# The first wide block of weights of a transformer kernel: its high part split between the roots and the tokens' high parts, its low part made by VectorE in four steps

## The reference

```python
h = jnp.concatenate([meta, x], axis=1)          # 16 + 512 tokens, 1024 wide
xn = rmsnorm(h, ln1_w[l])
proj = xn @ w_in[l]
dq, dk, dv, gq, gk, gv, gr, zf, zb = jnp.split(proj, splits, axis=-1)
log_g_f = jax.nn.log_sigmoid((zf @ gla_gate_w2_f[l] + gla_gate_b_f[l]).astype(f32)) / GLA_TAU
go = gla_bidirectional(gq * GLA_DK ** -0.5, gk, gv, log_g_f, log_g_b)
```

## Time and profile before

| | us |
|---|---|
| median of three executions | 2353.7 |
| lowest, highest | 2352.68, 2358.15 |
| the profiled execution | 2351.1 |
| span of its instructions | 2349.8 |
| PE busy in it | 2178.6 (93%) |
| DVE, ACT, POOL busy | 1522.6, 896.7, 739.2 |

### The profile page before, as it was taken

The page is one execution under the profiler, slowest core; times in us unless marked ns, Lnnn a source line. Parts: engine busy times, 40 slices in busy tenths (PEclk is TensorE's granted clock), DMA queues, the critical chain, the costliest instruction groups (busy, mean ns, idle before and its releaser), DMA issues.

```text
span 2349.8 us, 31219 instructions
## 1 busy us (share of the span) xinstructions
PE 2178.6 (93%) x12667; PEld 1270.3 (54%) x12743; DVE 1522.6 (65%) x2554; ACT 896.7 (38%) x1066; POOL 739.2 (31%) x548
## 2 busy tenths in 40 slices
PE   5999889888999988999999999999979988999998
PEld 3565554455565555777656555555545455444444
DVE  2557663338979999999578888888868174433002
ACT  4433452333333423666433333333333354444110
POOL 4311001311414342322123333334417401544540
PEclk8999899998999999999999999999979999999999
DMA  5114562215868777778899999999721311232300
GB/s 195 66 46 144 179 213 74 91 37 197 319 245 290 269 275 256 290 289 310 301 361 375 376 383 379 379 384 371 271 101 61 106 55 36 72 108 108 143 36 36
DMA packets 194479, 483.39 MB, mean 206 GB/s; under 512 B 10672, under 2 KB 93648, under 8 KB 188320
## 3 DMA queue, kind: packets, MB, share of 16 engines
q1 hardware_dynamic: 154624, 334.65, 40.1%
q0 software_dynamic: 39712, 146.74, 16.5%
HBM read 428.92 MB, written 52.43 MB: 205 GB/s over the span
## 4 chain that ended last, share of the span: by engine, by line
PE 54%; DVE 24%; DMA 14%; ACT 3%; issue 3%; POOL 2%; SPq 1%; DVEq 0%; ACTq 0%; POOLq 0%
PE psum L559 14%; PE psum L560 14%; PE psum L558 14%; DMA expert_act<-act_dram 11%; DVE weight_low L1968 6%; DMA rows_b<-peer_v_dram,row_index 2%; DVE row_sum L2197 2%; PE psum L956 2%; POOL weight_low L2518 2%; PE psum L748 1%; DVE hidden_low L2364 1%; DVE rows_a L2184 1%; DVE rows_b L2184 1%; DVE expert_act L2359 1%; PE psum L839 1%
## 5 line engine op out<-in xcount | busy, mean ns | idle before, releaser
L558 PE MATMUL psum<-x_high,weight_high 128*128 128x384 bf16 (+3 forms) x1826 | 640.7, 351 | 39.9 <-DVE weight_low L1968 24.1
L559 PE MATMUL psum<-x_low,weight_high 128*128 128x384 bf16 (+3 forms) x1845 | 647.3, 351 | 12.1 <-DVE x_low L1859 5.9
L560 PE MATMUL psum<-x_high,weight_low 128*128 128x384 bf16 (+3 forms) x1844 | 645.5, 350 | 0.6
L1270 ACT ACTIVATE weight_high<-weight_stage 128x4096 bf16<-128x4096 f32 (+2 forms) x100 | 356.2, 3562 | 241.7 <-PE psum L560 129.1
L2518 POOL TENSOR_TENSOR weight_low<-weight_stage,weight_high 128x512 bf16<-128x512 f32 (+1 forms) x237 | 308.8, 1337 | 431.3 <-ACT weight_high L1270 431.3
L558 PE MATMUL psum<-hidden_high,weight_high 128*128 128x384 bf16 x1024 | 335.4, 328 | 10.0 <-DVE hidden_low L2364 10.0
L559 PE MATMUL psum<-hidden_low,weight_high 128*128 128x384 bf16 x1024 | 335.4, 328 | 0.0
L560 PE MATMUL psum<-hidden_high,weight_low 128*128 128x384 bf16 x1024 | 335.3, 327 | 0.0
L1968 DVE TENSOR_TENSOR weight_low<-weight_stage,weight_high 128x4096 bf16<-128x4096 f32 x69 | 304.8, 4417 | 36.2 <-ACT weight_high L1270 36.2
L558 PEld LDWEIGHTS psum<-x_high,weight_high 128*128 128x128 bf16 (+1 forms) x1856 | 186.2, 100 | 210.8 <-DVE weight_low L1968 28.6
L560 PEld LDWEIGHTS psum<-x_high,weight_low 128*128 128x128 bf16 (+1 forms) x1856 | 185.9, 100 | 158.9 <-issue 13.4
(11 more groups left out here) (349 smaller groups left out, 2969.9 us busy)
## 6 DMA issues: line engine op xcount, KB each, us to landing
weight_stage<-peer_u_dram SPq DMA_DIRECT2D x32, 2048.0 KB, 8.6
weight_stage<-peer_v_dram SPq DMA_DIRECT2D x32, 2048.0 KB, 11.6
weight_stage<-mlp_w_dram SPq DMA_DIRECT2D x16, 2048.0 KB, 8.0
weight_stage<-ada_w_dram SPq DMA_DIRECT2D x12, 2048.0 KB, 8.0
act_dram<-norm_value SPq DMA_DIRECT2D x128, 192.0 KB, 10.1
gate_dram<-gate_matrices SPq DMA_DIRECT2D x12, 2048.0 KB, 12.2
gates<-gate_dram SPq DMA_DIRECT2D x32, 768.0 KB, 16.7
expert_act<-act_dram SPq DMA_DIRECT2D x32, 768.0 KB, 18.5
```

What stands on the lines that cost most here:

```text
L558: self.nc.tensor.matmul(out, left[0], right[0], start=first, stop=False)
L559: self.nc.tensor.matmul(out, left[0], right[1], start=False, stop=False)
L560: return self.nc.tensor.matmul(out, left[1], right[0], start=False, stop=last)
L1270: nc.scalar.activation(k.block_view(m.w_high, n % SPLITS, n), k.block_view(m.w_stage, n % STAGES, n), ACT.Copy).then_inc(*s.w_high.up(n))
```

## The change

ACT now splits block 1 between the roots and the tokens' high parts. The low part of block 1 is DVE's: four subtractions of 128x8x128, one for each column group, the first ahead of DVE's share of z, the other three behind it. PE waits for one group at a time: a new counter `first_low` for groups 0 to 2, `w_low[1]` for the last. The functions of the diff besides `first_low` are `by_vector`, PE's and ACT's `column_tiles`, ACT's `norm` and DVE's `projections`.

```diff
+        self.first_low = self.new("first_block_split")
     def by_vector(self, n):
-        return (self.block["da_q"] <= n <= self.block["da_v"] or ...
+        return (n == self.block["gla_qk"] or self.block["da_q"] <= n <= self.block["da_v"] or ...
...
         m_rows = 2 * GLA_RANK if name == "z" else P
-        if f == 0:
+        if name == "gla_qk":
+            n = self.k.block[name]
+            self.nc.tensor.wait_ge(*(s.first_low.at(f) if f < 3 else s.w_low[1].at(n)))
+            self.block = (n,) + tuple(self.k.block_view(part, n % SPLITS, n) for part in (m.w_high, m.w_low))
+        elif f == 0:
             self.block = self.weights(name)
...
         if parts_free is not None:
             nc.scalar.wait_ge(*parts_free)
+        if j == "ln1":
+            self.split(k.block["gla_qk"])
         for t in range(KT):
             nc.scalar.wait_ge(*s.normed.at(j, t))
...
-        if f == 0:
+        if f == 0 and name != "z":
             self.begin(name)
...
-        self.column_tiles("z", 0)
+        for f in range(4):
+            self.first_low(f)
+            if f == 0:
+                self.column_tiles("z", 0)
...
+    def first_low(self, f):
+        nc, s, k, m = self.nc, self.s, self.k, self.m
+        n, at = k.block["gla_qk"], slice(P * f, P * (f + 1))
+        low, whole, high = (k.block_view(buffer, slot, n)[:, :, at] for buffer, slot in (
+            (m.w_low, n % SPLITS), (m.w_stage, n % STAGES), (m.w_high, n % SPLITS)))
+        nc.vector.wait_ge(*s.w_high.at(n))
+        nc.vector.tensor_tensor(low, whole, high, ALU.subtract).then_inc(
+            *(s.first_low.up(f) if f < 3 else s.w_low[1].up(n)))
```

More of the change, by code:

```diff
@@ L462, in by_vector @@
     def by_vector(self, n):
-        return (self.block["da_q"] <= n <= self.block["da_v"] or self.block["w_out", 0] <= n <= self.block["w_out", 1]
+        return (n == self.block["gla_qk"] or self.block["da_q"] <= n <= self.block["da_v"] or self.block["w_out", 0] <= n <= self.block["w_out", 1]
                 or self.block["u", 0] <= n <= self.block["v", NG - 1])
```

## The result

| us | before | after |
|---|---|---|
| median of six executions each | 2353.19 | 2339.73 |
| lowest, highest | 2348.94, 2358.15 | 2332.01, 2340.83 |
| the profiled execution | 2351.1 | 2340.46 |
| its span | 2349.8 | 2339.2 |

The ratio of the times is 0.9934, 95% interval 0.992 to 0.9949, so 12 to 19 us are gained. Two more measurements of the same kernel gave 0.9947 (0.9928 to 0.9965) and 0.9939 (0.9926 to 0.9952). The forecast was 2341, with 2336 to 2347.

A forecast was written before the change was run, and what follows sets the result against it. PE was taken as the bound (54% of the chain), pausing 10.4 us for POOL's weight_low; 9.8 (earlier start) + 1.5 (group 0's clock) + 1.0 (gates' clock) = 12.3 us off the 2353.7 median gives 2341, range 2336 to 2347.

The forecast's parts named there:

- The split at no cost: ACT's moved split runs from 18.9 to 22.5 us, costed at nothing, with some 0.2 us of cover for a late load.
- Rival A: Block 1's load lands late, at 24.1; first token tile 5.6 us late, gain 6.7, time 2347; 5%.
- The first step: DVE's first low-part step takes 1.22 us (bounds 1.1 to 2.8), so PE starts group 0 at 33.35, 9.8 us earlier.
- The other steps and POOL: DVE's three later steps end at 37.4, hidden by group 0 and gates; POOL's gla_v pieces end at 45.6, not 52.0.
- Group 0's clock: With the pause down to about 0.6 us, PE runs group 0 at full clock: 1.5 us gained.
- The gates' clock: Low clock in the gate products and group 1 costs 3.65 us; 1.0 counted back, ends -1.5 and +3.65.
- The sum: PE's earlier start plus both clock terms: 9.8 + 1.5 + 1.0 = 12.3 us, with ends of 8.3 and 15.
- B: Rival: the gain is taken back later at an engine PE doesn't feed; gain 0, time 2353.7; 7%.
- C: Rival: the 1.2 GHz clock holds through group 0, gates and groups 1 to 3; 9.2 us slower, 2363; 4%.
- D: Rival: PE waits for all four DVE steps and starts at 37.4; gain 8.2, time 2345.5; 2%.

The follow-up runs named there:

- experiment 7: Changed kernel with the two wide loads issued in the opposite order, block 2 first; 2345.48 us, ratio 0.9971.
- experiment 8: Changed kernel, gate products between group 1's steps, DVE's memset and small sum ahead of the norm, its first step in two halves; 2341.12 us, ratio 0.9947.
- experiment 2: Changed kernel without ACT's move: only DVE's four low-part steps against the kernel before; 2343.84 us, ratio 0.9958.
- experiment 3: Changed kernel, but DVE makes the low part in one instruction instead of four steps; 2345.52 us, ratio 0.9969.
- experiment 4: The changed kernel measured again, unaltered, beside the kernel before; 2339.02 us, ratio 0.9947.
- experiment 11: The changed kernel measured once more, unaltered, beside the versions with two rows of gate products; 2339.13 us, ratio 0.9939.
- experiment 5: Changed kernel with one gate product after each of the eight steps of column group 1; 2343.0 us, ratio 0.9954.
- experiment 10: Changed kernel, gate products in two rows, DVE's memset and small sum ahead of the norm, its first step in two halves; 2338.52 us, ratio 0.9932.
- experiment 1: Kernel before with only ACT's split of the first wide block moved; POOL still makes the low part; 2353.19 us, ratio 1.000.
- experiment 6: Kernel before, without the change, with the gate products between the steps of column group 1; 2352.23 us, ratio 1.000.
- experiment 9: Changed kernel with the gate products in two rows, ahead of column groups 1 and 2; 2339.75 us, ratio 0.9942.

## Why the prediction was right

- **The split at no cost.** Right in size, tight in cover. It started at 19.44, not 18.9, since the tokens and so the load's issue were 0.6 us later in that execution; 0.24 us of the chain was lost. The stated cover of 0.2 us past 18.9 is nearly what the runs show (0.3), and beyond it experiment 7 lost 5.0. Rival A is a true mechanism, priced too high: for a landing at 24.1 it gave 5.6 us, all by which the first token tile is late, where DVE's need of that tile, at 23.38, leaves 5.0. It came on its own only in small, 0.24 us in the first profile and 0.55 in that of experiment 8.
- **The first step.** 1.22 us from the line through two sizes; measured 1.20. PE started at 33.51 instead of 33.35, so 9.66 us and not 9.8. The bound of 2.8 us for a step beside POOL wasn't touched: POOL only issued loads from 32.33 on, and the step took what the others did. By the Trainium skill's rule on the shared ports ("SBUF — State Buffer", "SBUF: two separate sides") POOL's issues wouldn't block DVE; this trace agrees, 1.20 us for the step beside them and 1.20 for each of the later ones.
- **The other steps and POOL** were hidden as counted: 37.2 for the last step, 46.0 for POOL's pieces.
- **Group 0's clock.** 33.51 to 39.09 is 5.58 us against 6.95: 1.37 for the 1.5 predicted. Experiments 2 and 3 show what it rests on: z's wait of 0.45 and this one of 0.5 kept the clock in every profile, 2.6 and 3.7 lost it in the one profile of each. So the short wait is worth that too, and not only the 3 us that it saves.
- **The gates' clock** was the mis-sized term, and the most interesting. I took 1.0, a value between the ends of -1.5 and +3.65. The first profile gives 0.0 (gates 0.14 shorter, group 1 as much longer). The other two profiles of the change give +3.3, near the upper end. That end was some 0.3 too high, mostly since at full clock the row takes 3.76 us from its start to group 1 (38.77 to 42.53) and not 16 x 0.22 = 3.5. It isn't a term with a middle value but one that is there or not in an execution. 9.66 + 1.37 + 0 = 11.0 and 9.90 + 1.38 + 3.3 = 14.6 are the two sums.
- **The sum.** No profile gave the 12.3 us forecast: by the end of the run the three of the change were 10.7, 15.5 and 15.5 earlier. The ratios of the three measurements (in the order first, experiment 4, experiment 11) come to 15.5, 12.5 and 14.4 us, each with some 3 to 4.4 to either side, of which the profiles explain only the part that is made in the first 60 us. So that the median came within 1.3 us of 2341 is in part luck; the range and the mechanism are what was right. A slip in the chances doesn't touch it: no change was given 0.08 where B and half of A make 0.095.
- **Rivals B, C and D.** B: 10.7, 15.5 and 15.5 us are left at the end in the three profiles of the change. In experiments 5 and 10, 7.1 and 5.6 us were lost from 245 to 350 us, but the granted clock is enough for that: TensorE had 0.50 for 41 and 38 us of that stretch where the kernel before had it for 24. C: group 0 ran at full clock in every profile with the steps and the moved split. D: experiment 3 is what it would have been, 2345.52 measured for the 2345.5 given, but the agreement is luck: PE started at 36.44 and not at 37.4, since one step has one fixed part and z stood behind it; group 0 lost its clock, the 1.5 us of which the estimate had counted as gained; and the gates' 1.0 wasn't gained either. The profile was 6.7 us earlier at 95 us where 8.2 was given.

What stays open is the rest of the spread between executions. From 245 to 350 us the profiles go from 7.1 us lost (experiment 5) to 1.1 won (experiment 4) with the same instructions there and a different granted clock, and no kernel here tried to hold it. It also stays open why the clock falls in the gate products of one execution and not of the next.

## What to carry to other kernels

When PE waits for a chain of two engines, ask of each link what its engine has to do first: moving the first link alone gained nothing, since the second engine's program didn't reach its part sooner. Hand an operand over in the pieces in which the reader uses it, and the first of them short: here a wait of 0.5 us instead of 3.7 also kept TensorE's clock in the profiles, worth 1.4 us more. A step put ahead of a critical row takes on its own wait too, so look at when its load lands in several executions, not in one.

## What the runs showed that was not expected

- A row of sixteen float32 matmuls, 32 rows by 264 columns, lets the clock fall in some executions (4.57 us, and group 1 slow to 48 us) and not in others (3.82 us), with the same work in front. Over all profiles here with the row of sixteen, the clock fell in it or at its end in five of eight (the kernel before, experiments 1, 2 and 3, the change's first) and was kept in three (experiments 4, 7 and 11). With the products apart or in two rows of eight it never fell between group 0's return to full clock and 240 us, in five profiles (experiments 5, 6, 8, 9 and 10). Whether it is float32 or the 32 rows of the array that matters was not separated.
- Going from bfloat16 matmuls to two float32 ones and back costs 0.3 us: 1.42 us a step against 1.11 counted, eight times over. In experiment 5 it took 0.21 us from the last bfloat16 start to the first float32 one (39.23 to 39.44) and 0.64 from there to the next bfloat16 one (40.08), where 0.11 and 0.44 were counted.
- With the pause before group 0 at 2.63 us the clock was already down (one profile), at 0.46 it was not (six profiles).
